# Pre-norm factors applied to products instead of to inputs, in a single-core fp32 transformer kernel

## The chip, the core and the metric

The kernel runs on one core of a Trainium2 chip. A core has TensorE (PE: matmuls), VectorE (DVE), ScalarE (ACT), GpSimd (POOL) and SyncE (SP, which issues transfers here), each with its own queue; they meet through semaphores. The metric is device microseconds of one execution, median of the runs shown.

## The reference, cut to what matters

512 tokens of width 1024 pass an attention layer A, a feed-forward network, an attention layer B, a second feed-forward network, and then a second block (which the change does not touch).

```python
def rms_norm(x, g):
    y = x32 * lax.rsqrt(jnp.mean(x32 * x32, axis=-1, keepdims=True) + EPS)
    return (y * g.astype(jnp.float32)).astype(x.dtype)
...
mix = dilated_mixer(rms_norm(h, g[0]), w_qkv_a[l], ...)      # layer 0: q, k (rotated), v products
kvf = rms_norm(h, kv_norm) @ w_kvf                           # layer 1: k, v, forget gates
mix = fox_mixer(rms_norm(h, g[0]), w_q_b[j], ...)            # layer 1: q product
h = h + rms_norm(mix, g[1])                                  # post-norm
f = conv_ffn(rms_norm(h, g[2]), w_up[l], conv_w[l], conv_b[l], w_down[l])
h = h + rms_norm(f, g[3])                                    # post-norm
```

A norm that feeds a product (pre-norm) is a gain per feature times one factor per token. The factor, 1 / sqrt(mean square + eps), does not depend on the feature, so it commutes with a product over features. `conv_ffn` multiplies by `w_up`, runs a causal convolution of three taps over the tokens, adds a bias, gates (gelu of one half times the other) and multiplies by `w_down`.

## The kernel before, in words

Activations lie feature-major: eight tiles of 128 features x 512 tokens (h, 128x512 each, chunk k). Every product is made in three matmuls per block of 128x128 weights, high x high, high x low and low x high parts (`hi_lo_product`, L490 to L494, the matmuls of L493). GpSimd splits each weight unit (eight blocks) into its high and low parts (L482, L484) into one of three slots; a slot is free when the product that read it is complete. SyncE loads weight units into a ring of four. `fm_linear` makes feature-major chunks of 512 tokens into PSUM banks 0 to 3 in turn; the first three chunks of a stage are made together, chunk k of the input by chunk k, as it becomes ready (L523 to L529). `tm_linear` makes token-major blocks (the v products). All orders are written by hand, engine by engine; each wait is a semaphore count.

A seam between two stages, in layer A's output say, goes like this (`out_act`, `out_dve`, `out_pe`, L636 to L680). VectorE copies each output chunk from PSUM to mix (L667). ScalarE squares it (L592). VectorE adds the squares into one tile (L598), TensorE sums over partitions with a matmul by ones that leaves the sum on all partitions (L603), ScalarE takes the root (L614), VectorE the reciprocal of 128x512 (L619). Then VectorE makes mix * gain * factor (L674) and adds it to h (L678). ScalarE squares h chunk by chunk (L580), TensorE sums (L610, eight matmuls by ones), again root and reciprocal of 128x512 (L614, L619). VectorE multiplies h by gain and factor (L626), ScalarE rounds that to the high part (L499), VectorE takes the low part (L504), and the next product begins. The start of the kernel is the second half of this, for x.

In a feed-forward network (`ffn_pe`, `ffn_act`, `ffn_dve`) each half has 22 up chunks of 24 matmuls and then 8 down chunks of 33. ScalarE reads an up chunk's bank with the third tap's weight (L719), VectorE adds the two other taps from the same bank (L740, L743), which frees it; ScalarE takes the gelu (L726), VectorE multiplies (L749), ScalarE rounds (L499), VectorE takes the low part (L504). Down chunk 0 reads the 11 gated tiles in order as each low part comes. During the down products VectorE also accumulates a matrix-vector product for the second block (`mod_products`, L1194 and L1196), which TensorE sums with one-column matmuls (L1204).

Layer B (`mixb_*`) makes v in two halves of 96 matmuls (`b_v0`, `b_v1`), the gates (`b_f`, 24), the first pair of heads' keys and queries (`kq_part`, 48) and 18 matmuls of the next pair, and then runs 64 attention tasks. ScalarE evicts v (L1079), then rounds a constant table (L1082), then takes Exp and Ln of the gates (L1087, L1088), then evicts keys and queries (L1039). VectorE's scan of the gates and their split (L1112 to L1118) must be done before the first task.

## Time and profile before

| | |
|---|---|
| median of 3 runs | 2648.06 us (2647.53 to 2664.75) |
| the profiled execution | 2677.43 us, its span 2675.6 us |
| TensorE busy | 2373.2 us, 89% of the span, mean granted clock 0.919 |
| VectorE, GpSimd, ScalarE busy | 1394.8, 1105.0, 589.8 us |
| in the chain that ended last | PE 81%, DVE 14%, ACT 3% |

The chain that ended last is followed back from the last instruction; its shares say which engine the time was spent on. An engine's busy time says little here, since the seams in which one engine waits for another are short. The stretches to look at are the seams, at 259 to 310, 661 to 693, 1013 to 1064 and 1415 to 1441 us, and the start.

### The profile page before, as it was taken

How to read it: one execution, taken by the hardware profiler on the slowest of the kernel's cores; microseconds unless marked ns; L12 is line 12 of the kernel's file. 1: busy time of each engine (PE TensorE's matmuls, PEld its weight loads, DVE VectorE, ACT ScalarE, POOL GpSimd, SP SyncE). 2: the span in 40 equal slices, each digit the busy share in tenths (PEclk: the TensorE clock that was granted, in tenths of full speed). 3: DMA queues.
4: the chain of work that ended last, by engine and by line, in shares of the span. 5: the costliest groups of instructions: out<-in, count | busy, mean ns of one | idle time of the engine just before them, and what ended most of it. 6: DMA issues, size and time to landing. Idle time of an engine off the chain costs nothing.

```text
span 2675.6 us, 34115 instructions
## 1 busy us (share of the span) xinstructions
PE 2373.2 (89%) x14068; PEld 1901.7 (71%) x14068; DVE 1394.8 (52%) x2005; ACT 589.8 (22%) x1159; POOL 1105.0 (41%) x632
## 2 busy tenths in 40 slices
PE   7998799999799996999996989559688896899998
PEld 5866588887577774888883657448487895688886
DVE  4455657456733346474466430777945554550431
ACT  2052220121232222210211300302533221210110
POOL 4613367666342232667662204404110024456663
PEclk9999899999899998999996999769789768899999
DMA  4201125335121111334354101102010001222321
GB/s 154 95 24 48 48 95 176 108 103 193 48 71 40 40 45 42 102 136 143 101 173 178 38 3 58 54 1 80 31 49 3 2 1 55 66 92 95 106 91 63
DMA packets 54058, 204.12 MB, mean 76 GB/s; under 512 B 6000, under 2 KB 6128, under 8 KB 52880
## 3 DMA queue, kind: packets, MB, share of 16 engines
q1 hardware_dynamic: 52560, 188.34, 21.5%
q0 software_dynamic: 1344, 13.60, 1.3%
q8 instruction: 112, 1.84, 0.3%
q14 instruction: 42, 0.34, 0.0%
HBM read 197.72 MB, written 4.19 MB: 75 GB/s over the span
## 4 chain that ended last, share of the span: by engine, by line
PE 81%; DVE 14%; ACT 3%; issue 1%; POOL 1%; DMA 0%; DVEq 0%; SPq 0%; POOLq 0%; ACTq 0%
PE bank L493 59%; PE bank L781 3%; PE bank L809 2%; PE bank L610 1%; DVE nb L619 1%; PE bank L1359 1%; PE bank L1367 1%; PE bank L1339 1%; PE bank L2022 1%; PE bank L796 1%; DVE nb L1911 1%; PE bank L2277 1%; PE bank L2018 1%; PE bank L785 1%; DVE big L1902 1%
## 5 line engine op out<-in xcount | busy, mean ns | idle before, releaser
L493 PE MATMUL bank<-xn_r,parts_r 128*128 128x512 f32 (+1 forms) x3104 | 975.3, 393 | 48.1 <-DVE big_r L504 13.3
L493 PE MATMUL bank<-big_r,parts_r 128*128 128x512 f32 x3112 | 898.2, 392 | 1.0 <-POOL parts_r L484 1.0
L482 POOL TENSOR_SCALAR parts_r<-ring 128x1024 fp32r<-128x1024 f32 x297 | 337.1, 1135 | 1182.3 <-PE bank L493 1157.7
L484 POOL TENSOR_TENSOR parts_r<-ring,parts_r 128x1024 fp32r<-128x1024 f32 x297 | 743.3, 2503 | 24.8
L493 PEld LDWEIGHTS bank<-xn_r,parts_r 128*128 128x128 f32 x3104 | 589.1, 192 | 174.9 <-issue 41.6
L493 PEld LDWEIGHTS bank<-big_r,parts_r 128*128 128x128 f32 x3112 | 583.4, 189 | 123.4 <-DVE big_r L504 2.7
L740 DVE SCALAR_TENSOR_TENSOR big<-bank,small,big 128x511 f32<-128x511 f32 x88 | 65.9, 749 | 268.1 <-ACT big L719 268.1
L719 ACT ACTIVATE big<-bank,small 128x512 f32<-128x512 f32 x88 | 68.3, 781 | 488.3 <-PE bank L493 488.3
L2418 DVE TENSOR_TENSOR big<-big 128x512 f32<-128x512 f32 x32 | 82.2, 2573 | 70.5 <-ACT big_r L2399 70.5
L2372 DVE SCALAR_TENSOR_TENSOR h<-bank,vecs,h 128x512 f32<-128x512 f32 x24 | 17.8, 750 | 193.4 <-PE bank L493 193.4
L493 PE MATMUL bank<-parts_r,xn_r 128*128 128x384 f32 x352 | 95.2, 353 | 15.5 <-DVE big L1902 9.6
L2310 POOL TENSOR_TENSOR big<-big 64x384 f32<-64x384 f32 x12 | 9.9, 822 | 219.8 <-PE bank L2049 176.8
L868 DVE CUSTOM_DVE_ANT_0 big<-bank,cst 128x128 f32<-128x128 f32 (+3 forms) x112 | 54.4, 490 | 85.0 <-PE bank L785 48.8
L610 PE MATMUL bank<-nb,base 128*128 128x512 f32 x112 | 64.8, 717 | 36.4 <-ACT nb L580 36.3
L1196 DVE SCALAR_TENSOR_TENSOR big<-cst,vecs,big 128x1024 f32<-128x1024 f32 x42 | 93.5, 2252 | 2.3 <-DMA cst<-mod_w 1.2
L493 PE MATMUL bank<-mix_r,parts_r 128*128 128x512 f32 x224 | 89.6, 400 | 0.0
L781 PE MATMUL bank<-big 64*128 64x128 f32 (+3 forms) x224 | 81.0, 466 | 0.6 <-issue 0.6
L493 PEld LDWEIGHTS bank<-parts_r,xn_r 128*128 128x128 f32 x352 | 67.7, 201 | 17.9 <-DVE big L1902 10.2
L749 DVE TENSOR_TENSOR big<-big 128x512 f32<-128x512 f32 x44 | 79.6, 1808 | 0.8 <-ACT big L726 0.8
L1902 DVE SCALAR_TENSOR_TENSOR big<-bank,small,big 128x488 f32<-128x488 f32 (+5 forms) x108 | 68.3, 636 | 20.5 <-ACT big L1857 17.3
L610 PEld LDWEIGHTS bank<-nb,base 128*128 128x128 f32 x112 | 21.7, 220 | 80.0 <-issue 38.5
L809 PEld LDWEIGHTS bank<-big 128*128 128x128 f32 x560 | 72.6, 191 | 5.1 <-issue 0.4
(348 smaller groups left out, 3004.3 us busy)
## 6 DMA issues: line engine op xcount, KB each, us to landing
ring<-weights SPq DMA_DIRECT2D x297, 512.0 KB, 3.5
cst<-mod_w SPq DMA_DIRECT2D x48, 512.0 KB, 4.0
big<-consts POOLq DMA_DIRECT2D x1, 4096.0 KB, 15.9
cst<-consts SPq DMA_DIRECT2D x2, 1280.0 KB, 8.4
h<-x SPq DMA_DIRECT2D x8, 256.0 KB, 5.2
h_store<-h POOLq DMA_DIRECT2D x1, 2048.0 KB, 7.7
h<-h_store POOLq DMA_DIRECT2D x1, 2048.0 KB, 9.0
out<-mix SPq DMA_DIRECT2D x8, 256.0 KB, 2.2
```

The costliest lines, as they stand in the source:

```text
L482: pool.tensor_scalar(rounded(w_hi[:, slot]), w, 1.0, 0.0, ALU.mult, ALU.add).then_inc(sem("hi_ready"), 1)
L484: pool.tensor_tensor(rounded(w_lo[:, slot]), w, value(w_hi[:, slot]), ALU.subtract).then_inc(part_ready, 1)
L493: mm = pe.matmul(ps, rounded(w[a]), rounded(x[b]), start=(start and n == 0), stop=(stop and n == 2))
L610: pe.matmul(bank[7][:, :], ones, sq[:, k % 2], start=(k == 0), stop=(k == KD - 1)).then_inc(summed, 1)
L719: act.activation(cv[:, i % 4], bank[i % 4][:, :], ACT.Identity, bias=gain(f"cb{l}", 2 * KH * s + i), scale=gain(f"cw{l}2", 2 * KH * s + i))\
L740: link(dve, dve.scalar_tensor_tensor(out=c[:, 1:T], in0=ps[:, 0:T - 1], scalar=gain(f"cw{l}1", w), in1=c[:, 1:T], op0=ALU.mult, op1=ALU.add))
L749: dve.tensor_tensor(ff_lo[:, j - 1], ge[:, (j - 1) % 2], cv[:, (2 * j - 1) % 4], ALU.mult)\
L781: mm = pe.matmul(ps[:, 0:w], qT[r:r + HD, hd // 2 % ring, tb * P:(tb + 1) * P], kT[r:r + HD, hd // 2 % ring, 0:w], start=True, stop=(sel i ...
L809: mm = pe.matmul(ps[:, g * HD:(g + 1) * HD], PT[:, t % 2, g, kb * P:(kb + 1) * P], vT[:, kb, hd * HD:(hd + 1) * HD], start=(kb == 0), stop ...
L1196: ins = dve.scalar_tensor_tensor(out=acc, in0=w, scalar=c, in1=acc, op0=ALU.mult, op1=ALU.add)
L1902: ins = dve.scalar_tensor_tensor(out=u[:, :, o0:o1], in0=ps[:, :, o0 + s:o1 + s], scalar=gd_tap(kind, f, j), in1=u[:, :, o0:o1], op0=ALU.m ...
L2418: dve.tensor_tensor(ff2_lo[:, f], ff2_lo[:, f], ff2_lo[:, f], ALU.mult).then_inc(sem("mlp_sq"), 1)
```

## The change

- In a pre-norm, the factor no longer multiplies the inputs. Their high part is now h * gain, rounded (ScalarE, `feed_act`), their low part h * gain minus the high part (one VectorE operation, `feed_dve`); both depend on no root. The factor multiplies the products: layer A's rotation tables (and its v evictions, by a scale per token), each of the 88 up chunks in place in its PSUM bank (`scale`, VectorE), layer B's v evictions (ScalarE's scale), its gates, and its keys and queries (VectorE, where ScalarE took them out before).
- The sums of squares of h go to buffers of their own (eight tiles), and are summed later, after product chunk 1 (layer A), chunk 2 (feed-forward) or `b_v0` (layer B), by 32 one-column matmuls (`pre_sums_pe`) that leave a 128x4 column of token sums. Root and reciprocal work on 128x4. Four matmuls spread the column over all partitions as a row (`pre_spread_pe`), after the next chunk, and ScalarE copies it to SBUF.
- A post-norm sums over the squares with 8 one-column matmuls, root and reciprocal on 128x4, and a spread of four matmuls into bank 5, from which L674's successor reads the factor. The last square is no longer added by VectorE but summed by TensorE. The table of the root is loaded ahead of the last square.
- VectorE's loop over chunks of h becomes, per chunk: product, addition, low part of the chunk before.
- VectorE's order in the up phase: scale chunk i, then the taps of chunk i-1, then the gate or a low part. ScalarE's tap waits for the scale.
- In layer A the first chunk is made alone (`together=1`), and rotations come two chunks late. In layer B the gates' weights come between the halves of v, and the low parts of the query input are made after the factor's row.
- At the start, weight unit 0 is loaded right behind the small vectors, the base constants behind x's chunk 1, and unit 1 behind chunk 3.

```diff
-    out += [("b_v0", tm_units(wf[:, D:D + 512])), ("b_v1", tm_units(wf[:, D + 512:2 * D])),
-            ("b_f", fm_units(pad_cols(wf[:, 2 * D:], [P], B_HEADS))), ("b_kq", key_query),
+    out += [("b_v0", tm_units(wf[:, D:D + 512])), ("b_f", fm_units(pad_cols(wf[:, 2 * D:], [P], B_HEADS))),
+            ("b_v1", tm_units(wf[:, D + 512:2 * D])), ("b_kq", key_query),
...
+        PRES = ["a", "ffn0", "b", "ffn1"]
+        pre_sq = big[:, 6144:6144 + KD * T].rearrange("p (k t) -> p k t", k=KD)
+        pre_squared, pre_summed = sem("pre_squared"), sem("pre_summed")
+        pre_sd_ready, pre_rs_ready = sem("pre_sd_ready"), sem("pre_rs_ready")
+        pre_spread, pre_row = sem("pre_spread"), sem("pre_row")
+
+        def token_columns(pe, ps, cols):
+
+            for tb in range(TB):
+                mm = pe.matmul(ps[:, tb * P:(tb + 1) * P], cols[:, tb:tb + 1].broadcast_to((P, P)), ident, start=True, stop=True)
+            return mm
+
+        def pre_sums_pe(pe, st):
+            n = PRES.index(st)
+            ps = grab(pe, 7, pre_sd_ready, n + 1)
+            pe.wait_ge(pre_squared, (n + 1) * KD)
+            for tb in range(TB):
+                for k in range(KD):
+                    mm = pe.matmul(ps[:, tb:tb + 1], pre_sq[:, k, tb * P:(tb + 1) * P], ones[:, 0:1],
+                                   start=(k == 0), stop=(k == KD - 1))
+            mm.then_inc(pre_summed, 1)
...
+        def pre_spread_pe(pe, st):
+            n = PRES.index(st)
+            ps = grab(pe, 7, pre_row, n + 1)
+            pe.wait_ge(pre_rs_ready, n + 1)
+            token_columns(pe, ps, pre_rs).then_inc(pre_spread, 1)
...
+            act.activation(pre_sd, bank[7][:, 0:TB], ACT.Sqrt, bias=gain("eps"), scale=1.0 / D).then_inc(pre_sd_ready, 1)
...
+            dve.reciprocal(pre_rs, pre_sd).then_inc(pre_rs_ready, 1)
...
+            act.activation(rstd, bank[7][:, :], ACT.Copy).then_inc(pre_row, 1)
...
+        def squares_added(act, st, ready, k, ready0=0):
+            n = POSTS.index(st)
+            if k == KD - 1:
+                act.activation(norm_cols[:, 16:17], gain("eps"), ACT.Sqrt)
+            act.wait_ge(*after(ready, ready0 + k + 1))
+            if k >= 3:
+                act.wait_ge(post_added, ADDS * n + k - 2)
+            act.activation(sq[:, k % 2] if k else var, mix[:, k], ACT.Square).then_inc(post_squared, 1)
+
+        def add_squares(dve, st, k):
+            n = POSTS.index(st)
+            dve.wait_ge(post_squared, n * KD + k + 1)
+            if k > 1:
+                dve.wait_ge(post_added, ADDS * n + k - 1)
+            dve.tensor_tensor(var, var, sq[:, k % 2], ALU.add).then_inc(post_added, 1)
...
+        def post_rstd_pe(pe, st):
+
+            n = POSTS.index(st)
+            ps = grab(pe, 5, *after(st + "_tmp", KD))
+            pe.wait_ge(post_added, ADDS * (n + 1))
+            for tb in range(TB):
+                pe.matmul(ps[:, tb:tb + 1], var[:, tb * P:(tb + 1) * P], ones[:, 0:1], start=True, stop=False)
+                if tb == 0:
+                    pe.wait_ge(post_squared, (n + 1) * KD)
+                mm = pe.matmul(ps[:, tb:tb + 1], sq[:, 1, tb * P:(tb + 1) * P], ones[:, 0:1], start=False, stop=True)
+            mm.then_inc(sem("post_sum"), 1)
+            pe.wait_ge(sem("post_col_rs"), n + 1)
+            token_columns(pe, ps, col_rs).then_inc(sem("post_rs"), 1)
...
+        def feed_act(act, src, g, hi, k, ready, done):
+
+            act.wait_ge(*ready)
+            act.activation(rounded(hi[:, k]), src[:, k], ACT.Copy, scale=gain(g, k)).then_inc(sem(done), 1)
+
+        def feed_dve(dve, src, g, hi, lo, k, ready, done):
+            dve.wait_ge(*ready)
+            dve.scalar_tensor_tensor(out=rounded(lo[:, k]), in0=src[:, k], scalar=gain(g, k), in1=value(hi[:, k]),
+                                     op0=ALU.mult, op1=ALU.subtract).then_inc(sem(done), 1)
+
+        def feed_squares(act, g, x, name, ready):
...
+                feed_act(act, h, g, x[0], k, ready(k), name + "h")
+                act.activation(pre_sq[:, k], h[:, k], ACT.Square).then_inc(pre_squared, 1)
...
-            rstd_recip(dve, st)
+            post_rstd_dve(dve, st)
             dve.wait_ge(*after(st + "_mix", 2 * KD if half == 1 else KD))
             for k in range(KD + 1):
                 if k < KD:
-                    dve.scalar_tensor_tensor(out=tmp[:, k % 2], in0=mix[:, k], scalar=gain(g, k), in1=rstd,
+                    dve.scalar_tensor_tensor(out=tmp[:, k % 2], in0=mix[:, k], scalar=gain(g, k), in1=bank[5][:, :],
                                              op0=ALU.mult, op1=ALU.mult).then_inc(sem(st + "_tmp"), 1)
-                if k:
-                    dve.wait_ge(*after(st + "_tmp", k))
-                    dve.tensor_tensor(h[:, k - 1], h[:, k - 1], tmp[:, (k - 1) % 2], ALU.add).then_inc(sem(st + "_h"), 1)
-                    dve.wait_ge(*after(st + "_h", k))
-            rstd_recip(dve, st + "n")
+                    dve.wait_ge(*after(st + "_tmp", k + 1))
+                    dve.tensor_tensor(h[:, k], h[:, k], tmp[:, k % 2], ALU.add).then_inc(sem(st + "_h"), 1)
+                if k and feed:
+                    fg, (hi, lo), name = feed
+                    feed_dve(dve, h, fg, hi, lo, k - 1, after(name + "h", k), name + "l")
+            dve.wait_ge(*after(st + "_h", KD))
+            if not feed:
+                rstd_recip(dve, st + "n")
...
+            def scale_rows(f):
+                if f == PARTS - 1:
+                    pre_sums_pe(pe, st)
+                if f == PARTS:
+                    pre_spread_pe(pe, st)
...
+            pre_recip_dve(dve, st)
+            dve.wait_ge(pre_row, PRES.index(st) + 1)
+
+            def scale(s, i):
+                dve.wait_ge(*after(f"{st}_up{s}", i + 1))
+                dve.tensor_tensor(bank[i % 4][:, :], bank[i % 4][:, :], rstd, ALU.mult).then_inc(sem(st + "_sc"), 1)
+
+            def conv(s, i):
...
+
+            def gated(s, j):
+                dve.wait_ge(*after(st + "_gelu", KH * s + j + 1))
+                dve.wait_ge(*after(st + "_conv", 2 * KH * s + 2 * j + 2))
+                dve.tensor_tensor(ff_lo[:, j], ge[:, j % 2], cv[:, (2 * j + 1) % 4], ALU.mult).then_inc(sem(st + "_ff"), 1)
+
             for s in range(2):
...
+                for i in range(2 * KH + 6):
+                    j, odd = divmod(i, 2)
+                    if i < 2 * KH:
+                        scale(s, i)
+                    if 1 <= i <= 2 * KH:
+                        conv(s, i - 1)
+                    if not odd and 2 <= j <= KH + 1:
+                        gated(s, j - 2)
+                    if odd and 3 <= j <= KH + 2:
+                        split_dve(dve, ff_lo, ff_hi, ff_lo, j - 3, after(st + "_ffh", KH * s + j - 2), st + "_ffl")
+                out_dve(dve, st, g, feed, half=s, then=lambda f, s=s: mod_products(dve, l, s, f))
...
+            def between(f):
+                if f == 1:
+                    pre_sums_pe(pe, "a")
+                if f == 2:
+                    pre_spread_pe(pe, "a")
+                if f >= 2:
+                    rotate(f - 2)
...
+            tm_linear(pe, "b_v0", 512, token_blocks(b_xkv), TB, "b_va", "b_vt", ready="b_xkvl")
+            pre_sums_pe(pe, "b")
...
+            pre_spread_pe(pe, "b")
+            tm_linear(pe, "b_v1", 512, token_blocks(b_xkv), TB, "b_vb", "b_vt", read0=TB)
...
+            pre_sqrt_act(act, "b")
+            act.wait_ge(pre_rs_ready, PRES.index("b") + 1)
+            for i in range(TB):
+                take_v(i)
+            pre_row_act(act, "b")
+            for k in range(KD):
+                feed_act(act, h, "g10", b_x[0], k, after("ffn0_h", k + 1), "b_xnh")
...
+            for i in range(TB, 2 * TB):
+                take_v(i)
...
-            for c in range(2):
-                kq_take(act, c)
...
+            for c in range(2):
+                kq_take(dve, c)
...
+                    unit(0)
+                if k == 1:
                     const(base[:, :], "base", 3 * P, small_in)
-            for u in range(n_units):
+                if k == 3:
+                    unit(1)
```

VectorE, end of the up phase of a feed-forward half, before: the last two chunks' taps, then gate and low part in turn; then the down phase begins (L1194, L667).

```order
L740 SCALAR_TENSOR_TENSOR big<-bank,small,big 128x511
L743 SCALAR_TENSOR_TENSOR big<-bank,small,big 128x510
L740 SCALAR_TENSOR_TENSOR big<-bank,small,big 128x511
L743 SCALAR_TENSOR_TENSOR big<-bank,small,big 128x510
L749 TENSOR_TENSOR big<-big 128x512
L504 TENSOR_TENSOR big_r<-big,big_r 128x512
L749 TENSOR_TENSOR big<-big 128x512
L504 TENSOR_TENSOR big_r<-big,big_r 128x512 x2
L1194 TENSOR_SCALAR big<-cst,vecs 128x1024 x2
L667 COPY mix<-bank 128x512
```

The same place in the change (L821 scale, L826 and L829 taps, L836 gate, L507 low part):

```order
L821 TENSOR_TENSOR bank<-bank,nb 128x512
L826 SCALAR_TENSOR_TENSOR big<-bank,small,big 128x511
L829 SCALAR_TENSOR_TENSOR big<-bank,small,big 128x510
L507 TENSOR_TENSOR big_r<-big,big_r 128x512
L826 SCALAR_TENSOR_TENSOR big<-bank,small,big 128x511
L829 SCALAR_TENSOR_TENSOR big<-bank,small,big 128x510
L836 TENSOR_TENSOR big<-big 128x512
L507 TENSOR_TENSOR big_r<-big,big_r 128x512
L836 TENSOR_TENSOR big<-big 128x512
L507 TENSOR_TENSOR big_r<-big,big_r 128x512 x2
L1308 TENSOR_SCALAR big<-cst,vecs 128x1024 x2
```

The first row waits for the last up chunk, and both pairs of taps, which stood half before it, now stand behind it, with one more low part between them.

TensorE, seam between layer A and the first feed-forward network, before: the last rows of the down side, then the two kinds of sums.

```order
L603 MATMUL bank<-nb,base 128x512
L610 MATMUL bank<-nb,base 128x512 x8
```

The same place in the change (L667 and L670 one-column sums, L609 the spread; the eight sums of L610 have no counterpart here, their successor of 32 stands three up chunks later):

```order
L667 MATMUL bank<-base,nb 128x1
L670 MATMUL bank<-base,nb 128x1
L667 MATMUL bank<-base,nb 128x1
L670 MATMUL bank<-base,nb 128x1
L667 MATMUL bank<-base,nb 128x1
L670 MATMUL bank<-base,nb 128x1
L667 MATMUL bank<-base,nb 128x1
L670 MATMUL bank<-base,nb 128x1
L609 MATMUL bank<-base,norm_cols 128x128 x4
```

Nine full-width matmuls have gone from between the last output chunk and the first up chunk; twelve small ones stand there.

## Rows read from the trace of the kernel before

**Rows 1.** The page, the chain that ended last by engine.

```profile
PE 81%; DVE 14%; ACT 3%; issue 1%; POOL 1%; DMA 0%; DVEq 0%; SPq 0%; POOLq 0%; ACTq 0%
```

**Rows 2.** That chain in time, first long seam: start us, us, what.

```profile
256.43 2.78 DVE nb L598
260.50 2.73 DVE nb L598
263.36 2.06 PE bank L603 x2
266.17 3.36 DVE nb L619
...
289.25 16.66 PE bank L493 x66
...
309.69 165.39 PE bank L493 x720
```

**Rows 3.** VectorE's timeline in that seam: start us, us, instruction.

```profile
271.61 0.75 DVE L674 SCALAR_TENSOR_TENSOR nb<-mix,small,nb 128x512 f32<-128x512 f32 x1
272.27 0.68 DVE L678 TENSOR_TENSOR h<-h,nb 128x512 f32<-128x512 f32 x1
...
297.45 0.25 DVE L1176 RECIPROCAL vecs<-vecs 128x16 f32<-128x16 f32 x1
```

**Rows 4.** Windows: stretch, length, busy of each engine, then granted clock.

```profile
258.90:263.30 4.40, 0.14 (x1) 0.00 (x0) 3.62 (x3) 1.91 (x2) 3.38 (x2) 0.80 0.37 119
...
309.60:312.00 2.40, 2.31 (x6) 1.86 (x7) 1.60 (x3) 0.00 (x0) 2.32 (x2) 0.50 0.62 155
...
474.90:478.40 3.50, 3.50 (x34) 3.49 (x32) 0.69 (x1) 0.00 (x0) 3.08 (x2) 1.00 0.09 36
```

**Rows 5.** TensorE's timeline at one-column matmuls (two records each).

```profile
474.91 3.63 PE L1204 MATMUL bank<-base,big 128*128 128x1 f32 x32
```

**Rows 6.** Timeline of all engines, end of an up phase (down begins 414.55).

```profile
414.55 9.16 PE L493 MATMUL bank<-big_r,parts_r 128*128 128x512 f32 x38
...
416.01 2.40 POOL L484 TENSOR_TENSOR parts_r<-ring,parts_r 128x1024 fp32r<-128x1024 f32 x1
...
417.02 1.95 DVE L749 TENSOR_TENSOR big<-big 128x512 f32<-128x512 f32 x1
...
421.61 1.90 PEld L493 LDWEIGHTS bank<-big_r,parts_r 128*128 128x128 f32 x9 [0.25 <-DVE big_r L504]
```

**Rows 7.** VectorE's groups by form: count, busy us, mean ns.

```profile
L665 DVE TENSOR_TENSOR mix<-mix,bank 128x512 f32<-128x512 f32 x16 | 11.0, 687 | 35.7 <-PE bank L493 35.7
```

**Rows 8.** Timelines of TensorE, VectorE and ScalarE, head of layer B.

```profile
692.92 24.60 PE L493 MATMUL bank<-parts_r,big_r 128*128 128x512 f32 x96 [8.05 <-DVE big_r L504]
720.77 22.01 PE L493 MATMUL bank<-parts_r,big_r 128*128 128x512 f32 x96 [3.24 <-ACT big L1079]
...
763.11 0.48 PE L781 MATMUL bank<-big 64*128 64x128 f32 x2
...
671.82 1.42 DVE L674 SCALAR_TENSOR_TENSOR nb<-mix,small,nb 128x512 f32<-128x512 f32 x2
...
758.89 0.68 DVE L1118 TENSOR_TENSOR nb_r<-nb,nb_r 16x512 fp32r<-16x512 f32 x1
...
743.31 1.91 ACT L1082 ACTIVATE cst_r<-cst 128x2048 fp32r<-128x2048 f32 x1
...
751.94 0.63 ACT L1088 ACTIVATE nb<-nb 16x512 f32<-16x512 f32 x1
```

**Rows 9.** The chain in time, seam into the second block.

```profile
1420.03 3.36 DVE nb L619
...
1437.56 3.37 DVE nb L619
```

**Rows 10.** The start: GpSimd's timeline (first weights split), and the chain.

```profile
12.73 1.04 POOL L482 TENSOR_SCALAR parts_r<-ring 128x1024 fp32r<-128x1024 f32 x1 [12.28 <-DMA ring<-weights]
...
46.37 5.78 PE bank L493 x24
```

More of the change, by code:

```diff
@@ L431, in build @@
         stat = sb("stat", 64)
+        norm_cols = sb("norm_cols", 32)
+        col_sd, col_rs, pre_sd, pre_rs = (norm_cols[:, 4 * n:4 * n + 4] for n in range(4))
         BIG = 20992
@@ L504, in split_dve, with fm_linear @@
             dve.tensor_tensor(rounded(lo[:, k]), x[:, k], value(hi[:, k]), ALU.subtract).then_inc(sem(done), 1)
-        def fm_linear(pe, name, chunks, kt, x, full, read, ready=None, then=None, full0=0, read0=0):
+        def fm_linear(pe, name, chunks, kt, x, full, read, ready=None, then=None, full0=0, read0=0, together=PARTS):
             u0 = UNITS[name]
@@ L620, in rstd_recip @@
             dve.wait_ge(rstd_ready, n)
-        def norm_dve(dve, g, hi, lo, st):
-            for k in range(KD + 1):
-                if k < KD:
-                    dve.scalar_tensor_tensor(out=lo[:, k], in0=h[:, k], scalar=gain(g, k), in1=rstd,
-                                             op0=ALU.mult, op1=ALU.mult).then_inc(sem(st), 1)
-                if k:
-                    split_dve(dve, lo, hi, lo, k - 1, after(st + "h", k), st + "l")
-        def norm_act(act, hi, lo, st):
+        PRES = ["a", "ffn0", "b", "ffn1"]
@@ new lines, in post_rstd_act, with post_rstd_dve @@
+        def post_rstd_act(act, st):
+            act.wait_ge(sem("post_sum"), POSTS.index(st) + 1)
+            act.activation(col_sd, bank[5][:, 0:TB], ACT.Sqrt, bias=gain("eps"), scale=1.0 / D).then_inc(sem("post_sd"), 1)
+        def post_rstd_dve(dve, st):
+            n = POSTS.index(st)
+            dve.wait_ge(sem("post_sd"), n + 1)
+            dve.reciprocal(col_rs, col_sd).then_inc(sem("post_col_rs"), 1)
+            dve.wait_ge(sem("post_rs"), n + 1)
+        def feed_act(act, src, g, hi, k, ready, done):
+            act.wait_ge(*ready)
+            act.activation(rounded(hi[:, k]), src[:, k], ACT.Copy, scale=gain(g, k)).then_inc(sem(done), 1)
@@ L658, in out_dve @@
                     then(f)
-                if f >= 2 and half != 0:
+                if f >= 2 and f < KD and half != 0:
                     add_squares(dve, st, f - 1)
@@ new lines, in ffn_dve @@
+            pre_recip_dve(dve, st)
[4 more added lines that the diff above has]
+            def conv(s, i):
+                ps, c, w = bank[i % 4], cv[:, i % 4], 2 * KH * s + i
+                dve.wait_ge(*after(st + "_tap", w + 1))
+                link(dve, dve.scalar_tensor_tensor(
+                    out=c[:, 1:T], in0=ps[:, 0:T - 1], scalar=gain(f"cw{l}1", w), in1=c[:, 1:T],
+                    op0=ALU.mult, op1=ALU.add))
+                dve.scalar_tensor_tensor(
+                    out=c[:, 2:T], in0=ps[:, 0:T - 2], scalar=gain(f"cw{l}0", w), in1=c[:, 2:T],
+                    op0=ALU.mult, op1=ALU.add).then_inc(sem(st + "_conv"), 1)
@@ L938, in mixa_pe @@
             pe.wait_ge(small_in, 32)
-            for k in range(KD):
-                sum_squares(pe, "in", k)
             def rotate(f):
```

205 lines of the change are left out of this document (90 added, 115 removed).

## The prediction

> **What bounds the kernel now.** I read the page's chain by engine first: TensorE holds 81% of it, VectorE 14% [rows 1]. So the end is set by TensorE in the products and by VectorE in the seams, and a change to the norms acts in the seams. There the chain in time shows the order of work [rows 2]: a slow addition of squares (2.73), a ones-matmul at low clock (2.06), a reciprocal of 128x512 (3.36), the loop over h, a second such reciprocal, and then 72 matmuls (66 of them in one piece) before a wait of 2.4 for GpSimd's next unit, until up chunk 3 starts at 309.69. The down and up products themselves run 720 matmuls in 165.39 us, 0.23 each, with no wait worth naming. I then read the windows for TensorE's clock [rows 4], the timelines of the three long seams and of the start, and the group of the VectorE form nearest to the added one [rows 7]. The profiled execution took 2677.43 us, of which the span is 2675.6; that is 29 us above the median of 2648.06. I sum changes on the trace and take them off the median.
>
> **Post-norm, four seams.** In the first seam the last square ends at 260.47, when the addition starts [rows 2]. All but that square are added by 259.2 (256.43 + 2.78), so TensorE's one-column sums can start. One such matmul takes 0.22: 16 of them (32 records) filled the stretch of 3.5 us [rows 4, 5]. Seven remain after the square: 1.6, and some 0.4 more if the clock falls, as it did in 258.9 to 263.3 (mean 0.80) [rows 4]. Root and reciprocal on 128x4: 0.25 each, by the reciprocal of 128x16 [rows 3]. The spread, four small matmuls of two passes: 0.22 to 0.5 each, so 0.9 to 2.0, I take 1.9. With hand-overs VectorE starts its loop at about 265.3, where now it starts at 269.5 (266.17 + 3.36): 4.2 us sooner.
>
> **The loop and the head of the up phase.** Per chunk VectorE now does product, addition behind it, and low part. The first two are 0.75 and 0.68 [rows 3]; the new form has three SBUF operands and a gain like L674, so 0.75 too. With their overlaps 2.07 per chunk. ScalarE's rounding and square, 0.63 each [rows 8], fit beside. The first low part is there 3.6 us after the start, at 268.9; three chunks per k take TensorE 2.0 at full clock, so it is nowhere starved. Its 72 matmuls took 17.8 from 289.25, clock rise included [rows 2]: 286.8. Before, 307.1.
> Then come, on TensorE's path: 32 one-column sums, 7.0 (0.22 each), under which GpSimd's split of the next unit hides; chunk 3, 5.5; the spread, 1.1; and then nothing until bank 0 is free, since scaling begins only with the factor's row: copy 0.6, scale 0, scale 1, and two taps of 0.75. For the scale in place in PSUM no row writes PSUM from VectorE. The nearest is L665, one PSUM and one SBUF input, 0.687 [rows 7]; from below 0.25, a small operation's whole cost [rows 3], from above 2.9 (an operation held behind GpSimd for its whole 2.4 [rows 6]). I take 0.69. Chunk 4 then starts at 304.2, some 3.9 after the spread. A wait of 2.4 us had put the clock at 0.50 for 3 us [rows 4] and cost 1.1 of the 2.1 by which the 720 matmuls exceed 0.2268 each [rows 2]; I add that: 305.3. Before, chunk 4 started 5.4 + 1.1 after 309.69, at 316.2. **10.9 us gained** in this seam, and the same in the third (1013 to 1064), which repeats it.
>
> **The end of each up half, four times.** VectorE's order puts scale of chunk 21 ahead of the taps of chunk 20. Down chunk 0 writes bank 0, which those taps free. Now it starts at 414.55 without a wait; after the change, scale 0.69 and two taps 1.5 stand between: start at 416.95. Behind them a low part waits for GpSimd, which runs until 418.4 (the gate at 417.02 took 1.95 for that reason [rows 6]); then taps, gate, low, gate, low, low, to 423.6. Chunk 0 ends near 424.5, where now it ends at 422.6, after a last wait of 0.25 [rows 6]: 1.9, and up to 1.1 of clock for an idle stretch of 2.4. **2.5 us lost each, 10 in all.** In the middle of the up phase VectorE needs per chunk 0.69 + 1.5 + the gate or low part behind GpSimd, to 4.4 of 5.4 us; nothing is late there.
>
> **Layer B.** The seam starts 5 us sooner at the loop (671.82 [rows 8] to 666.8; mod sums on TensorE come first), one addition waits for GpSimd (1.3), and v starts after two low parts, at 673.6 instead of 692.92: 19.3 gained. From there to the first attention task it now takes 70.2 (to 763.11), with a wait of 3.24 for ScalarE's eviction in it [rows 8]. That wait goes. Added are the sums, 7.0, the spread, 1.1, and a new wait: ScalarE now holds the last v evictions before the table rounding (1.91), Exp and Ln with their table loads, and VectorE evicts the keys only behind the scan. From the end of v that is 0.7 + 1.9 + 3.8 on ScalarE (Exp and Ln at 0.63, and a table load before each, which I put at twice that, an estimate), then 6.3 on VectorE (Ln ended 752.57, the split 759.57 [rows 8]) and 0.7 for the eviction: 13.4, while TensorE has 10.9 of products: 2.5, and 0.6 of clock. 70.2 - 3.2 + 7.0 + 1.1 + 3.1 = 78.2, so 8.0 given back: **11.3 gained**. The evictions moved to VectorE inside the attention, 14 x 0.69, lie beside TensorE and cost nothing while VectorE is under half busy there; if that cover fails, they cost up to 9.7.
>
> **Last seam and start.** In the last seam GpSimd is done and the additions are fast, so what goes is the reciprocal (3.36), the ones-matmul and one fast addition, some 5.4, against 3.1 of sums, roots and spread at full clock: the loop starts 2.3 sooner than 1423.4 (1420.03 + 3.36), and the second reciprocal, now at 1437.56 [rows 9], 2.5 sooner. **2.5 gained.** At the start GpSimd has its first weights at 12.73 [rows 10]; they come about 6 us sooner, and chunk 0 can go as x arrives. But VectorE's low parts now fall into GpSimd's first three splits, each operation waiting one out: chunk 0 ends at 19 (never held) to 23 (held in turn). Then chunk 1, sums, chunk 2, spread and one rotation, with one clock rise: chunk 3 starts at 40 to 44.4, against 46.37 [rows 10], one rotation (0.9) still owed. **2.0 gained**, between 1 and 5.
> The Trainium skill ("SBUF — State Buffer", section "SBUF: two separate sides") says that a VectorE operation with two SBUF inputs and a GpSimd operation lock each other out for a whole instruction. Row L749 agrees (1.95, ended with GpSimd's 2.40) [rows 6].
>
> **Sum.** 10.9 x 2 - 10 + 11.3 + 2.5 + 2.0 = 27.6. 2648.06 - 27.6 = **2620.5 us**. The largest single price is the four strings of sums, 28 us in all, taken by the row [rows 5]. The Trainium skill ("TensorE: Matmul & The Clock Gate", section "Back-to-back issue gap") puts a matmul of 1 to 64 columns at about 60 cycles; by an estimate from that page alone the strings would take 6 to 7 us and the kernel about 2599. By the row it is nine times as much per matmul, so the page's figure is no part of the sum.
>
> **Rivals.**
> A, *the waits are longer*: the bank wait at up chunk 4 and those at the ends of the up halves each cost the clock more than once, or VectorE's loop is slowed. Gain of 5 to 20, 2628 to 2643. For it: both waits are new and at places without slack, and 0.50 follows a wait of 2.4 [rows 4]. Against: each is bounded by operations that have rows. Chance 0.23.
> B, *the clock falls in the strings of sums*: a string now runs at full clock [rows 4], but for 3.5 us only; the new ones are twice as long, with one column at a time. If the clock falls in them, a string takes 14 in place of 7 and the next chunk loses 1.5: 8.5 x 4 = 34 lost, 2654.5, slower than before. It decides from 6.9 us per string on. Against: 1.00 over the whole string, and full pace behind it. Chance 0.10; with A at its worst on top, slower by over 1% (0.04).
> C, *cheap sums, or the clock stays up*: at half the 0.22 a string saves 3.5, 14 in all; a clock that holds across the shorter gaps saves 1.1 at each of seven waits, 8. Together or apart 7 to 21 more, 2599 to 2613. Against: 0.22 is measured in the same form [rows 5]. The page's rule above is the extreme of the first. Chance 0.17.
> D, *the scale in PSUM is held or slow* (2.9 each): VectorE then needs over 5.4 per chunk and TensorE follows it, 88 x 0.7 to 1.2 = 60 to 100 lost, 2680 to 2720. Against: L665 ran at 0.687 beside GpSimd at work. Chance 0.04.
> The forecast, 2614 to 2628: 0.46.
>
> **Numbers.** The range reaches to C's lower half and to A's upper end: 2602 to 2643; B and D are left out. A measurement of this kernel can tell 1%, 26.5 us, from no change; my forecast lies just past that. Faster by over 1% (below 2621.6): C and somewhat over half of the forecast, 0.46. Within 1%: the rest of it, A and most of B, 0.45. Slower: D and the worst of B, 0.09.
>
> **What would show it.** In the changed profile: the first L674 successor at about 265 after 258.9 (5 to 6.5 us after the last matmul); 32 one-column matmuls in 7 us at granted clock 1.00; TensorE waiting 3 to 4 us before up chunk 4 for VectorE's second tap; 2.4 us of idle before each down phase; the scale's mean at 0.69; v of layer B starting 12 us after the last down matmul; ScalarE's Ln ending 6 us after v. Wrong would be: clock 0.5 within the sums, a scale mean over 1.5, or idle TensorE inside the up phase.

## The result, and the profile after

The changed kernel took 2687.43 us (median of 14 runs, 2671.17 to 2723.62), the kernel before beside it 2664.76 (14 runs). The ratio is 1.0089, 95% interval 1.0058 to 1.0120: 24 us **slower**. Forecast were 2620.5 on a base of 2648.06, a ratio of 0.9896, so 51 us at that base have to be explained. Ratios, here and below, leave out executions more than 1.5% above the fastest of the same kernel. The profiled execution took 2690.64 us.

First the page of the changed kernel: span, busy time, the chain by engine and line, and the groups of the products and of the new scaling (the columns of [rows 7] with the idle time before them).
```profile
span 2688.8 us, 34765 instructions
PE 2415.7 (90%) x14380; PEld 1943.1 (72%) x14380; DVE 1456.6 (54%) x2068; ACT 580.1 (22%) x1151; POOL 1102.9 (41%) x632
...
PE 83%; DVE 12%; ACT 3%; issue 1%; POOL 1%; DMA 0%; SPq 0%; DVEq 0%; POOLq 0%; ACTq 0%
PE bank L496 61%; PE bank L877 3%; PE bank L905 2%; PE bank L618 2%; PE bank L1453 1%; PE bank L1473 1%; PE bank L892 1%; PE bank L2136 1%; PE bank L1481 1%; DVE nb L2025 1%; PE bank L2132 1%; PE bank L881 1%; DVE big L2016 1%; PE bank L212
...
L496 PE MATMUL bank<-big_r,parts_r 128*128 128x512 f32 x3112 | 928.2, 402 | 12.5 <-DVE big L829 8.9
...
L821 DVE TENSOR_TENSOR bank<-bank,nb 128x512 f32<-128x512 f32 x88 | 61.3, 699 | 178.6 <-PE bank L496 160.4
```
VectorE gave up 2 points of the chain, TensorE took them ([rows 1] had 81 and 14). The scaling (L821) has the 0.69 that I gave it. But the products themselves, the same 3112 of them, have a mean of 402 ns where the kernel before has 392: that is no seam.

The chain in time through the first long seam of the changed kernel, the answer to [rows 2]:
```profile
264.06 2.85 DVE nb L659
...
270.34 0.19 DVE norm_cols L682
270.53 0.04 issue
270.57 2.09 PE bank L609 x8
272.66 0.02 issue
272.69 0.76 DVE nb L741
...
276.46 18.84 PE bank L496 x72
295.31 11.31 PE bank L618 x64
306.62 7.79 PE bank L496 x24
314.40 0.91 PE bank L609 x8
...
318.29 0.76 DVE big L829
319.05 0.04 issue
319.10 10.94 PE bank L496 x35
```
The windows of the same kernel over that string of sums and chunk 3 (stretch, length, busy time of each engine, granted clock; columns as in [rows 4]):
```profile
295.30:297.60 2.30, 2.30 (x24) 2.30 (x22) 0.00 (x0) 0.00 (x0) 2.30 (x2) 0.98 0.02 7
297.60:302.00 4.40, 4.40 (x22) 4.40 (x22) 0.00 (x0) 0.00 (x0) 4.32 (x3) 0.50 0.36 119
302.00:306.60 4.60, 4.60 (x23) 4.60 (x23) 0.00 (x0) 0.00 (x0) 2.36 (x2) 0.50 0.54 190
306.60:311.20 4.60, 4.60 (x12) 3.63 (x12) 0.18 (x1) 0.26 (x1) 0.00 (x0) 0.50 0.10 38
311.20:314.40 3.20, 3.20 (x16) 2.62 (x16) 0.00 (x0) 0.00 (x0) 0.00 (x0) 1.00 0.00 0
```
At first a sum takes 0.22 from start to start (two records each), as [rows 5] said. After 2.4 us, 11 of the 32 sums, the clock is granted at 0.50 (1.2 GHz) though TensorE is never idle, a sum takes 0.43, and the low clock reaches 4.6 us into chunk 3. The Trainium skill ("TensorE: Matmul & The Clock Gate", section "HAM oscillation — how this bites in real kernels") tells of idle gaps as what brings the clock down; these rows have none.

Stages, each from the start of its first product to that of the next stage, and the two gaps from the start of the last product ahead to the first behind, in us. B's attention counts from its first product at 766.4 in the kernel before, 3.3 behind the mark that the prediction used. The "place corrected" column is experiment 7 below, which differs in nothing but where one tile lies.

| stage | before | forecast | after | after, place corrected |
|---|---|---|---|---|
| start to layer A's v products | 104.2 | 102.2 | 110.9 | 110.4 |
| last output product of A to up chunk 0 | 30.6 | 10.3 | 10.0 | 10.1 |
| up chunk 0 to up chunk 4 | 27.4 | 36.4 | 42.6 | 42.2 |
| up chunk 4 to down chunk 0 (432 products) | 98.0 | 100.4 | 104.0 | 103.3 |
| last down product to v of layer B | 32.0 | 12.7 | 13.0 | 12.3 |
| v to the first product of B's attention | 73.5 | 81.5 | 87.9 | 86.2 |
| the perceptron's 1464 products | 333.7 | 333.7 | 341.3 | 333.8 |

The two gaps on which the change was meant to act shrank as forecast. The loss is in the strings and at the start, behind the waits, and in products that the change doesn't touch.

### The profile page after: what moved, and what is told of

Its sections match the earlier page's. It is cut to its first block, busy times and chain, and to the rows that moved or that the text cites. A ratio compares the mean times of both kernels' runs of the same rounds, so it can differ in the third digit from the quotient of the medians.

```text
span 2688.8 us, 34765 instructions
## 1 busy us (share of the span) xinstructions
PE 2415.7 (90%) x14380; PEld 1943.1 (72%) x14380; DVE 1456.6 (54%) x2068; ACT 580.1 (22%) x1151; POOL 1102.9 (41%) x632
## 4 chain that ended last, share of the span: by engine, by line
PE 83%; DVE 12%; ACT 3%; issue 1%; POOL 1%; DMA 0%; SPq 0%; DVEq 0%; POOLq 0%; ACTq 0%
PE bank L496 61%; PE bank L877 3%; PE bank L905 2%; PE bank L618 2%; PE bank L1453 1%; PE bank L1473 1%; PE bank L892 1%; PE bank L2136 1%; PE bank L1481 1%; DVE nb L2025 1%; PE bank L2132 1%; PE bank L881 1%; DVE big L2016 1%; PE bank L2121 1%; PE bank L588 1%
## 5 line engine op out<-in xcount | busy, mean ns | idle before, releaser
L496 PE MATMUL bank<-xn_r,parts_r 128*128 128x512 f32 (+1 forms) x3104 | 998.3, 400 | 50.1 <-DVE mix_r L693 14.2
L496 PE MATMUL bank<-big_r,parts_r 128*128 128x512 f32 x3112 | 928.2, 402 | 12.5 <-DVE big L829 8.9
L485 POOL TENSOR_SCALAR parts_r<-ring 128x1024 fp32r<-128x1024 f32 x297 | 333.8, 1124 | 1229.4 <-PE bank L496 1209.6
L496 PEld LDWEIGHTS bank<-xn_r,parts_r 128*128 128x128 f32 x3104 | 597.4, 194 | 191.3 <-issue 41.3
L496 PEld LDWEIGHTS bank<-big_r,parts_r 128*128 128x128 f32 x3112 | 594.4, 192 | 150.8 <-DVE big L829 10.6
L821 DVE TENSOR_TENSOR bank<-bank,nb 128x512 f32<-128x512 f32 x88 | 61.3, 699 | 178.6 <-PE bank L496 160.4
L2532 DVE TENSOR_TENSOR big<-big 128x512 f32<-128x512 f32 x32 | 87.1, 2724 | 73.1 <-ACT big_r L2513 73.1
L507 DVE TENSOR_TENSOR big_r<-big,big_r 128x512 fp32r<-128x512 f32 x76 | 105.9, 1395 | 0.4
L836 DVE TENSOR_TENSOR big<-big 128x512 f32<-128x512 f32 x44 | 83.8, 1905 | 0.0
L949 ACT ACTIVATE big<-big,stat 128x128 f32<-128x128 f32 (+3 forms) x112 | 62.0, 555 | 74.5 <-DVE stat L971 74.4
```

What stands on the lines that cost most here:

```text
L485: pool.tensor_scalar(rounded(w_hi[:, slot]), w, 1.0, 0.0, ALU.mult, ALU.add).then_inc(sem("hi_ready"), 1)
L496: mm = pe.matmul(ps, rounded(w[a]), rounded(x[b]), start=(start and n == 0), stop=(stop and n == 2))
L507: dve.tensor_tensor(rounded(lo[:, k]), x[:, k], value(hi[:, k]), ALU.subtract).then_inc(sem(done), 1)
L836: dve.tensor_tensor(ff_lo[:, j], ge[:, j % 2], cv[:, (2 * j + 1) % 4], ALU.mult).then_inc(sem(st + "_ff"), 1)
L949: act.activation(sbt, sbt, ACT.Exp, bias=nm(t + 1), scale=HD ** -0.5, accum_out=ls(t + 1)[:, g:g + 1]).then_inc(s("probs"), 1)
L2532: dve.tensor_tensor(ff2_lo[:, f], ff2_lo[:, f], ff2_lo[:, f], ALU.mult).then_inc(sem("mlp_sq"), 1)
```

## The experiments

Ratios are to the kernel before, run beside each on the same chip, with 95% intervals. "Less" or "more" in us is against the changed kernel's 2685.02 in experiment 1.

**1. The changed kernel again** (no edit).

> The changed kernel once more, nothing edited. In its first profile 96 back-to-back matmuls took 22.40 us in long stretches at granted clock 1.00, also in the unchanged multilayer perceptron of block 2, where the kernel before took 21.76. Theory P (a property of that one execution): the pitch of the perceptron comes back near 21.76, or changes again in other places, and the ratio to before stays 1.005 to 1.012. Rival Q (the scaling in PSUM or anything else of the change slows every matmul): 22.40 comes back in the same places. Losses of place that should repeat in either case: about 11 us for a string of one-column sums, 7 to 8 us for the chunk behind it, 2.6 us of idle before each down phase, chunk 3 of layer A's products at about 50 us.

Measured: 1.0083 (1.0053 to 1.0114). Theory P fails: the perceptron again has the slow pitch (341.3 for its 1464 products), so it is no property of one execution. The losses in the seams repeat too: strings of 9.1 to 10.8 (9.7 to 11.3 in the first execution), chunk 3 of layer A at 46.4 (49.4), 2.6 us from product to product ahead of each down phase. One thing doesn't repeat, and experiment 4 comes back to it: the clock's fall behind those last waits. To compare pitches I sum over a trace the part above 0.2267 of every distance between successive products that lies in 0.220 to 0.245. This excess is 28.8 and 28.6 us in the two executions, 2.0 in the kernel before.

**2. Sums as matmuls of 512 columns**
```
-            for tb in range(TB):
-                for k in range(KD):
-                    mm = pe.matmul(ps[:, tb:tb + 1], pre_sq[:, k, tb * P:(tb + 1) * P], ones[:, 0:1], ...)
+            for k in range(KD):
+                mm = pe.matmul(ps[:, :], rounded(ones_r[:, :]), rounded(pre_sq[:, k]), ...)
```
(squares written rounded; root and reciprocal on 128x512; in layers A and B four matmuls of the factor's row with one column of the identity give the columns back).

> The 32 one-column sums of each pre-norm are replaced by 8 matmuls of 512 columns with a matrix of ones, on squares rounded for a single pass; root and reciprocal then run on 128x512, with no spread in the feed-forward networks; in the two attention layers four one-column matmuls take the factor back to columns. Theory T (the granted clock falls in a string of one-column matmuls, and stays low in the next chunk): a string goes from 9.7 to 11.3 us to 1.8, the chunk behind it from 7.2 to 8.4 to 5.5, the spread goes in two places; root 0.7 and reciprocal 3.4 hide beneath the chunk. 12 to 13 us less in each feed-forward network, 8 to 10 in each layer: 40 to 46 us less than the changed kernel, ratio to before about 0.992. Rival R (the strings cost their 7 us at full clock and the loss is elsewhere): 5.2 us less per string, 20 to 23 us less in all, ratio to before about 1.000.

Measured: 2638.01 us, 0.9906 (0.9875 to 0.9937), 47 us less than the changed kernel. Its chain in time:
```profile
286.10 1.85 PE bank L619 x8
287.95 0.02 issue
287.97 0.70 ACT nb L632
...
288.76 3.37 DVE nb L636
...
295.29 4.85 PE bank L497 x20
```
and its windows at the end of the sums and over chunk 3:
```profile
283.20:285.00 1.80, 1.80 (x10) 1.43 (x8) 0.00 (x0) 0.00 (x0) 0.15 (x1) 1.00 0.00 0
285.00:290.60 5.60, 5.03 (x22) 3.85 (x21) 1.84 (x1) 0.69 (x1) 5.43 (x4) 1.00 0.21 56
```
Eight sums take 1.85, the clock stays at 1.00, and even the reciprocal of 128x512 (3.37), which the change had gone to lengths to avoid, lies mostly beneath chunk 3. From up chunk 0 to chunk 4 it takes 28.6 us instead of 41.6 (experiment 1). The 47 us are near Theory T's 40 to 46 and twice Rival R's 20 to 23. Not all of it is the string: the last wait ahead of up chunk 4 is 1.4 instead of 4.1, and behind it the clock stays at 1.00, where the changed kernel has 0.50 for 6.8 us (the window below, and 315.7 to 322.5 in experiment 1). Nor does this run say which trait of the new sums matters, since their width, their number of passes and the length of the string change together.
```profile
319.10:324.60 5.50, 5.50 (x13) 4.34 (x14) 3.95 (x6) 3.47 (x4) 0.00 (x0) 0.50 0.26 90
```

**3. Each string run twice** (`for tb in range(2 * TB)`, with `tb %= TB`).

> Every string of 32 one-column sums is run twice, the second time over the first one's result, so the output is unchanged. Theory T (clock falls in the string): the second half runs at half clock or goes in and out of it, 9 to 14 us more per string, 36 to 56 in all over the changed kernel. Rival R (0.22 us per matmul whatever the clock): 7.0 us more per string, 28 in all.

Measured: 2735.85, 1.0281 (1.0228 to 1.0335): 51 us more, 12.7 per string. One doubled string in the chain:
```profile
308.80 24.87 PE bank L619 x128
333.67 7.90 PE bank L496 x24
```
The second 32 sums take 13.4, 0.42 each, with the granted clock at 0.50 from 311.1 to 338.4: the second half runs at half clock throughout. T again; R had 7.0 per string.

**4. Taps ahead of the next scaling**
```
-                    if i < 2 * KH:
-                        scale(s, i)
                     if 1 <= i <= 2 * KH:
                         conv(s, i - 1)
+                    if i < 2 * KH:
+                        scale(s, i)
```

> In the up phases VectorE's order has the taps of chunk i-1 ahead of the scaling of chunk i. Theory: the four waits of 2.6 us before the down phases' first matmul go, with the clock's fall behind them: 10 to 14 us less than the changed kernel. Rival: the release of bank 0 was not what held TensorE, or the gate of the last pair comes later instead and the wait moves to the end of down chunk 0: 0 to 4 us less.

Measured: 2669.38, 1.0023 (0.9990 to 1.0055), 16 us less. The end of an up phase in the changed kernel, chain in time, as answer to [rows 6]:
```profile
412.89 8.03 PE bank L496 x35
420.92 0.02 issue
420.94 0.70 DVE bank L821
421.64 0.66 DVE big L826
422.30 0.02 issue
422.32 0.76 DVE big L829
423.08 0.04 issue
423.12 6.92 PE bank L496 x22
```
A scaling and two taps stand between the last product and the first of the down phase, exactly as the prediction wrote them; in this experiment that gap is 0.23, no gap. The waits are 4 x 2.4 = 10, of which 0.5 each comes back as a wait within down chunk 0 (the second half of the Rival, in small). The clock gives the rest, or a part of it. Behind this wait the changed kernel's first execution had (first line, clock 0.58) 24 down products in 7.2 us, and in experiment 1 (second line, clock 1.00) in 5.7:
```profile
423.20:427.20 4.00, 4.00 (x11) 3.12 (x12) 3.96 (x5) 0.82 (x3) 1.37 (x1) 0.58 0.00 0
423.00:430.00 7.00, 7.00 (x30) 5.68 (x31) 6.87 (x9) 2.15 (x4) 1.45 (x1) 1.00 0.00 0
```
The clock fell behind all four waits of the first execution and behind none in experiment 1; in all six traces with this order (these two and experiments 2, 3, 7 and 8) behind 12 of 24, for about 1.6 us each time. That makes 8 + 3 = 11 us on average. The two ratios allow 4 to 28, so the measured 16 doesn't contradict it.

**5. The kernel before again**, for its pitch.

> The kernel before once more, nothing edited. In its first profile three products took 0.680 us nearly everywhere at granted clock 1.00, an excess of 2 us over the whole kernel; in the five profiles of the changed kernel and its variants they take 0.686 to 0.700 wherever the moving operand lies in the tile big, and in the unchanged perceptron too: an excess of 26 to 30 us. Theory S (the place of big in SBUF sets it): 0.680 again, excess 2. Rival P (a state of the chip at the time): 0.700 in places, excess up to 30.

Measured: one execution, 2664.56, excess 2.0 us. That agrees with Theory S.

**6. The kernel before, one tile moved**
```
+        unused = sb("unused", 32)
         BIG = 20992
         big = two_views("big", BIG)
```

> The kernel before with an unused tile of 32 columns allocated just ahead of big, where the changed kernel has its new tile norm_cols of 32 columns; every instruction is the same, and big lies 128 bytes per partition higher. Theory S (place of big): products in the up and down phases and the perceptron take up to 0.700 per three, 24 to 28 us more than before, ratio 1.009 to 1.011. Rival I (the changed instructions set it, or chance): ratio 0.999 to 1.001.

Measured: 2680.00, 1.0078 (1.0050 to 1.0107), excess 32.5 us. Not one instruction differs, and Rival I falls. The time grows by 21 us only, the excess by 30; this trace also has a higher mean granted clock (0.932, and 0.919 and 0.923 in the two of the kernel before). Whether the slower pitch brings that about is open.

**7. The changed kernel, the tile put back** (`norm_cols` allocated behind `big`).

> The changed kernel with the 32 columns of norm_cols allocated behind big instead of ahead of it, so that big lies where the kernel before has it; nothing else differs. Theory S: 24 to 28 us less than the changed kernel, ratio to before 0.998 to 1.000. Rival I: ratio as the changed kernel's, 1.008.

Measured: 2661.81, 1.0015 (0.9989 to 1.0041), excess 2.2 us. The perceptron's products as one piece of the chain: the kernel before, the changed one, experiment 6 and experiment 7.
```profile
2322.22 333.74 PE bank L493 x1464
```
```profile
2327.63 341.27 PE bank L496 x1464
```
```profile
2319.01 341.29 PE bank L494 x1464
```
```profile
2306.36 333.76 PE bank L496 x1464
```
The same 1464 products at the same granted clock of 1.00 take 7.5 us more wherever 128 bytes more lie ahead of `big`. Three products then take up to 0.700 in place of 0.680, in a fixed pattern (236, 234, 230 ns). Products that read nothing from `big` keep their pitch: layer A's chunks take 5.48 in the changed kernel and 5.49 before. So the changed kernel with this one line moved can't be told from the kernel before: the change as such gained nothing that can be told, its gains and losses in the seams being about equal, and what made it slower was the place of a tile.

**8. Sums between products, in the feed-forward networks**
```
                     for k in range(kt):
                         product(ps, f, k)
+                        if inside and f == PARTS:
+                            inside(k)          # 4 of the 32 sums
```

> In the feed-forward networks the 32 one-column sums no longer form a string: four of them stand behind every three products of up chunk 3; root, reciprocal and spread then come after the chunk with nothing above them. Layers A and B keep their strings. Theory T (the clock falls because the string has so few columns): chunk 3 with its sums takes 5.5 + 7 = 12.5 us at a granted clock mostly 1.00, where string and chunk took 18 to 19; the exposed root and reciprocal cost 0.6; 5 to 6 us less in each of two places, 10 to 12 in all, ratio to before 1.004. Rival R (a one-column matmul takes 0.35 wherever it stands): 18 us for both, 1 us more in all.

Measured: 2693.96, 1.0122 (1.0086 to 1.0159), 9 us more than the changed kernel. Neither Theory T (12.5 us for chunk and sums) nor Rival R (18) forecast this. The chain and two of the windows:
```profile
303.37 1.49 PE bank L496 x3
304.86 1.50 PE bank L782 x8
306.36 1.49 PE bank L496 x3
307.85 1.50 PE bank L782 x8
```
```profile
302.00:310.00 8.00, 8.00 (x31) 7.33 (x32) 0.00 (x0) 0.00 (x0) 2.36 (x2) 0.50 0.37 130
310.00:318.00 8.00, 8.00 (x32) 7.23 (x31) 0.00 (x0) 0.00 (x0) 0.00 (x0) 0.50 0.00 0
```
With half of the time in products of 512 columns the clock still stays at 0.50 for the whole of chunk 3: 23.6 us for products and sums, where string and chunk in a row took 19. TensorE had waited 2.8 us for GpSimd just ahead (297.69), a wait that the string hides in the changed kernel and that the kernel before has at its chunk 3 (309.69). There, with pure products, the clock was at 0.50 too [rows 4] and back at 1.00 from 312.7; here, with sums between the products, it stays at 0.50 until 332.3. So the low clock doesn't need an unbroken string. Whether the mixture alone would have brought it down, without the wait ahead, this run doesn't show. What helped in these runs was fewer small matmuls (experiment 2), not spreading them.

**9. The kernel before, `big` 256 bytes higher** (`unused` with 64 columns).

> The kernel before with an unused tile of 64 columns ahead of big: big lies 256 bytes higher per partition, where 128 bytes cost 21 us. Theory W (it matters where big lies within 256 bytes, or against the tiles of the weights within 256): three products take 0.680 everywhere, excess about 2 us. Rival X (any shift, or a wider pattern such as 512): 0.686 to 0.700 again, excess 20 to 32.

Measured: 2662.12 in one execution, excess 2.0, perceptron 333.75. Theory W holds.

**10. The kernel before, all tiles 128 bytes higher** (`unused` ahead of the first tile).

> The kernel before with an unused tile of 32 columns ahead of the first tile: all tiles lie 128 bytes higher, the weights' parts as well as the moving operands. Theory Y (it is the distance between the moving operand and the weights or between its two halves that counts): three products take 0.680, excess about 2 us. Rival Z (it is where the moving operand itself lies): 0.700 now everywhere, in layer A's products too, excess 32 to 45 us.

Measured: 2667.05 in one execution, excess 2.0, perceptron 333.72. Theory Y: no absolute place counts. What the slow cases share is the distance between the moving operand and the weights' halves in `parts`, within 256 bytes. The two halves of the activations can't be it, since the down phases read both from `big` and are slow too. In experiment 2 `big` lay 640 bytes higher, 128 more than a multiple of 256, with an excess of 26.5: the same rule. It is reached by elimination: `big` moved against every tile below it at once, and of those only `parts` is read by every slow matmul. No run moved `parts` alone, and only distances of 128, 256 and 640 bytes were measured.

**11. All corrections together**: 2, 4 and 7, and layer A's rotations one chunk behind the products instead of two:
```
-                if f >= 2:
-                    rotate(f - 2)
+                if f == 2:
+                    rotate(0)
+                if f >= 2:
+                    rotate(f - 1)
 ...
-            rotate(2 * KA - 2)
             rotate(2 * KA - 1)
```

> The changed kernel with the sums as 8 matmuls of 512 columns, the taps ahead of the next scaling, norm_cols behind big, and layer A's rotations issued one chunk behind the products instead of two, so that one is owed at the end and not two. Theory: the effects add up: 47 (sums) + 16 (order) + 23 (place) + 3 (a rotation with its wait) = 89 us less than the changed kernel's 2685, about 2596, ratio to before 0.976. Rival: they overlap, since each also moves the clock's falls: 60 to 75 less, ratio 0.982 to 0.987.

Measured: 2607.06 us, 0.9765 (0.9718 to 0.9812): it beats both kernels, the one before by 62 us, the changed one by 85 (1.0083 to 0.9765). The single effects are -0.0177, -0.0060 and -0.0068, and the rotation gives some 3 us (60.3 from layer A's spread to its v products, 62.9 in the changed kernel). They add up to it, and the Rival's overlap (0.982 to 0.987) lies just outside the interval. Layer A's v products start at 97.2 instead of 110.9.

**12. As 11, layer A's first two chunks fed together** (`together=2`).

> As the kernel with the four corrections, and layer A's first two chunks fed together, k by k, instead of the first alone. Theory: chunk 0 is paced by VectorE's low parts (1.56 each beside GpSimd), so TensorE has the time for chunk 1's products between them, and chunk 2 starts 2 to 4 us sooner. Rival: at the start the clock is at half and 48 products need 21 us at 0.45, and the second unit's split comes 3.9 us after the first: 0 to 2 us later.

Measured: 2603.00 us, 0.9766 (0.9721 to 0.9811). Chunk 2 starts at 29.3 instead of 31.4, so the theory holds for its place; 2 us are under what this comparison can tell.

## Why the prediction was wrong

Step by step, against the 51 us between forecast and result:

- **The place of the tiles: missing.** Every duration of a product came from the kernel before (0.2268 each), on the silent assumption that products which the change doesn't touch keep it. The change has a line that broke it (not among those printed above), `norm_cols = sb("norm_cols", 32)`, a new tile of 32 columns ahead of `big`, and I read past it. Measured: 0.0068 to 0.0078 of the time (experiments 7 and 6), 18 to 21 us.
- **"32 one-column sums, 7.0" and "chunk 3, 5.5": the price failed.** The row behind it is right until the clock falls, after 11 to 21 of the 32 sums (2.4 to 4.8 us). Rival B, to which I gave 0.10, is what happened: the sums took 9.7 to 11.3 with 7.2 to 8.4 for the chunk behind. From up chunk 0 to chunk 4 that is 5.2 to 6.8 more than forecast, twice, and 4.7 to 6.4 more in layer B. B named the right mechanism and overstated the string (14), since a third or more of it runs at full clock. It put the point from which the gain is gone at 6.9 us per string; the strings stayed just below it, so they alone took most of the gain and didn't make the kernel slower. What I held against B, "1.00 over the whole string", came from a string half as long, and from one execution: in the changed kernel's trace that same string (486.26, 3.63 in [rows 5]) took 4.62 with the clock falling in it. The "nine times as much per matmul" beside the sum sets two passes against a figure for one; against the prediction's own 6 to 7 us for the four strings, the row's 28 are some four times as much.
- **"2.5 us lost each, 10 in all": right mechanism, small price.** The wait is 2.4, as written. The clock falls behind it in half of the cases and then costs 1.6; I had allowed "up to 1.1" and put it into no sum. Removing the wait gave back 16 by the medians.
- **"I add that: 305.3", the clock behind the wait at up chunk 4: too small.** I added 1.1. With the place corrected it cost 2.9 (clock 0.50 for 6.8 us), and the row that I priced it from already had 1.5: the 24 products behind 309.69 took 6.94, not 5.44. This is a part of Rival A (0.23), which happened beside B.
- **The start, "2.0 gained": failed by 8.7 (6.3 in experiment 1).** Chunk 3 starts at 49.4 and 46.4 in the two executions, not at 40 to 44.4: the string and its clock again. And two rotations are owed at the end, not one, with a wait for VectorE between them, because an addition of two SBUF operands (107.76, 2.57 us where 0.69 is usual) stood beside GpSimd's split (107.43, 2.34). In the chain of the changed kernel:
```profile
106.14 0.87 PE bank L1041 x2
...
107.76 2.57 DVE big L1101
110.33 0.04 issue
110.37 1.12 PE bank L1041 x2
```
- **Right:** post-norm. The gap ahead of the up phase went from 30.6 to 10.0 (forecast 10.3), the one ahead of v from 32.0 to 13.0, the last seam gave 1.9 (2.5), and up chunk 4 started 5.1 after the last product of chunk 3, the spread included, by the chain that the prediction lists. Right too: the scaling at 0.70 and no cost of it in the middle of an up phase (432 products in 103.3 with the place corrected, of which 2.4 are the wait at the end and 2.9 low clock behind the wait at chunk 4); Rival D is out.

Together, in the trace with the place corrected and against the forecast: the start 8, from up chunk 0 to the down phase 9 and 8, layer B 5. With 0 to 6 for the clock behind the four last waits and 18 to 21 for the place this is 48 to 57 us, against the 51 to be explained. A closer match would be chance, since the clock's falls differ from one execution to the next. What stays open: what in TensorE makes the distance of two operands count, and what in small matmuls brings its clock down. Neither was taken apart further.

## What to carry to other kernels

Price a run of small matmuls at the low clock once it is longer than the run in the row that you price it from, and look for a form with wide columns: eight single-pass matmuls of 512 columns did in 1.85 us what 32 of one column did in 11. Price the clock from more than one execution: behind the same wait it fell in one trace and not in the next. When a change allocates a tile, compare the distance of every matmul's two operands within 256 bytes before and after, and when a product that nobody touched has another mean, look there first. A reordering that lets an operation in ahead of the one that frees a buffer costs its wait, and often the clock behind the wait.

## What the hardware showed

- With `big`, and so the moving operand, 128 bytes per partition further from the weights (640 as well, 256 not), three matmuls of 512 columns take up to 0.700 us in place of 0.680. The levels lie between 0.687 and 0.700, and in the up phases they differ from one execution to the next (0.687 and 0.700 in the first two). It holds with the roles exchanged: layer B's v products, whose weights come from `big` and whose moving operand from `parts`, are slow as well (0.2333 each in experiment 1, 0.2268 before).
- A one-column matmul of two passes takes 0.22 at a granted clock of 1.00 and 0.43 at 0.50, so in these strings it scales with the clock. The Trainium skill ("TensorE: Matmul & The Clock Gate", section "Back-to-back issue gap") puts 1 to 64 columns at about 60 cycles, 0.025 us at the full clock; no run here comes near it, and the measured figure decides.
- In all eight strings of the changed kernel's two traces the granted clock fell to 0.50 with TensorE busy all the time, after 11 to 21 of 32 one-column matmuls. In experiment 8 it had fallen behind a wait and stayed at 0.50 for 34 us; in the first 23 of them TensorE spent as much time in 512-column products as in sums.
- The same wait of 2.4 us was followed by a clock of 0.50 in 12 of 24 cases, and by 1.00 in the others.
